# Sixteen of 31 convolution taps on TensorE in 32x32 tiles, on copies of the input turned by partitions

## The chip, the cores and the metric

One NeuronCore of a Trainium2 chip runs the whole program. The metric is the device time of one execution, in microseconds (us). Before the change it is 2149.69 us, the median of three runs (2148.77 to 2149.78).

## What is computed

Two stacked transformer blocks of different kinds, each two layers deep, over 256 tokens of width 1024, all in float32. What bears on the change is the mixer of the second block: its input projection gives queries, keys, values, a convolution input `c` (two halves of 512 channels) and gates. The convolution is depthwise, with 31 taps over the tokens, and a layer norm and a silu follow.

```python
        q, k, v, c, g = jnp.split(u @ w_in[i], splits, axis=-1)
        ...
        c = depthwise_conv(c, conv_w[i], conv_b[i])     # 31 taps, 512 channels, padding 15 on both sides
        c = jax.nn.silu(layer_norm_2(c, conv_ln_g[i], conv_ln_b[i]))
        y_conv = c @ w_conv_out[i]
        ...
        h = h + (g_attn * y_attn + g_conv * y_conv) @ w_o[i]
```

The input of the taps is the gated product of the two halves of `c`.

## The kernel before

Activations lie with features on the partitions and the 256 tokens along the free dimension, 128 features to a tile. Weights stream from HBM in blocks of eight 128x128 tiles (`raw`, 512 KB). Seven blocks are loaded ahead by SP; ScalarE rounds a block to its high half (`hi`), five blocks ahead of TensorE, and VectorE subtracts for the low half (`lo`), four ahead. A projection of 128 rows takes three matmuls for each weight tile (lo by high input, hi by high input, hi by low input).

The order of all work is written out by hand: `main_order` lists items, and every engine's program walks the same list. Side work is woven in by `Flow`: after each block of eight tiles, each engine calls `tick`, which takes one step ("next" to "next") of every chain that runs beside the main work. `tick` goes over the chains last in, first out; `chain(..., True)` puts one at the other end. The chains in this stage are the convolution (`conv2_steps`) and the attention (`att2_steps`: two pairs of heads, each scores, maxima, exponentials, division, transposes called `turn`, and `out`). In a chain's step every engine does its own part, so a step's place is tied to a block number on all engines.

In the second block's mixer the items are `c` 0 to 3 (each two columns of tiles), `conv2` (starts the chain after `c` 2), `c last`, `rcol`, `qkv` 0 to 2, `v2`, `qk norm`, `attention2` (starts that chain), eight `gate2`, four `attn out`, four `conv out`, four `wo`. VectorE makes the gated input, `Cb` (four tiles of 286 columns, zeros at both ends), from ScalarE's tanh. `CV` = 20 of the 31 taps are done on VectorE, one scalar_tensor_tensor of 256 columns each, accumulated in `cacc`. The other 11 are done on TensorE: ScalarE scales the identity by a tap's weights (`diag`, a ring of eight), TensorE multiplies the shifted `Cb` tile by it in float32 and accumulates in bank 4, and VectorE adds the bank to `cacc` (`conv sum`). A tick in the convolution chain has two taps on VectorE for each of two tiles, three diagonals on ScalarE, and three taps on TensorE, for two pairs of tiles in turn. Then come the mean, squares, variance, norm, silu and split, one tick each.

The attention of this stage uses the PSUM banks `ATT2` = (5, 6, 7, 2); the main items use `MAIN` = (0, 1, 3). A bank is waited for when it is taken (`take`) until its last reader has freed it.

In the first block, `quarters` multiplies in 64x64 tiles. It is quoted since the prediction reads its rows:

```python
                    for n in range(4):
                        for g, s in ((0, 0), (0, 1), (1, 0), (1, 1)):
                            rows, into = (slice(64 * t, 64 * t + 64) for t in (s, s ^ g))
                            h = 2 * n + g
                            i = pe.mm(outs[g][into, n * w:(n + 1) * w], left(h, rows), right(h, rows), True, True)
```

## Time and profile before

| | |
|---|---|
| median of three runs | 2149.69 us |
| the profiled execution | 2149.16 us, span 2147.4 us |
| TensorE matmul busy | 2120.1 us (99%) |
| VectorE busy | 1680.6 us (78%) |
| ScalarE busy | 1265.4 us (59%) |
| GpSimd busy | 13.1 us (1%) |
| DMA | 415 MB, mean 193 GB/s |

PE is TensorE's matmul, PEld its weight load, DVE VectorE, ACT ScalarE, POOL GpSimd, SP the engine that issues most DMAs. Times in rows are microseconds from the span's start unless marked ns; L198 and the like are lines of the kernel, and since helpers record every operation, a row is told by its tiles. A matmul's record goes on to the end of its pipeline, so that records overlap, and rates are read from start to start. "x6" in a timeline row is six instructions merged.

### The profile page before, as it was taken

The page shows a single profiled execution, that of the slowest core. Times are in us where ns is not written, and L with a number is a line of the kernel's source. Part 1 is how long each engine was busy: PE and PEld are TensorE (multiplying, and loading weights), DVE is VectorE, ACT ScalarE, POOL GpSimd, SP SyncE. Part 2 cuts the span into 40 slices and gives each one's busy share as a digit, 9 for nine tenths or more (in the row PEclk, how much of TensorE's full clock was granted, in tenths as well). Part 3 has the DMA queues.
Part 4 walks back from the last instruction along what each step waited for, and adds up shares of the span by engine and source line. Part 5 has one row for each costly group of instructions (what it writes and reads, how often), then busy time and mean ns, then how long its engine had stood idle before and what let it go on. Part 6 is the DMA issues. An engine that isn't in the chain of part 4 may idle for free.

```text
span 2147.4 us, 38873 instructions
## 1 busy us (share of the span) xinstructions
PE 2120.1 (99%) x16094; PEld 1934.2 (90%) x16094; DVE 1680.6 (78%) x2642; ACT 1265.4 (59%) x2122; POOL 13.1 (1%) x20
## 2 busy tenths in 40 slices
PE   8999999999999999999999999999999999999999
PEld 7898989999998899998888999888898889998888
DVE  7888698887877698776886677887688767878875
ACT  4765556555855755555655567665466545766554
POOL 0000000000000000000000000000000000000000
PEclk9999999999999999999999999999999999999999
DMA  9555577777644477555555533555555553346554
GB/s 371 192 194 174 173 244 258 240 244 276 215 158 168 158 253 231 186 186 186 180 193 187 168 117 132 203 191 191 187 177 191 192 186 128 124 164 205 191 191 129
DMA packets 116371, 415.12 MB, mean 193 GB/s; under 512 B 13105, under 2 KB 16561, under 8 KB 115682
## 3 DMA queue, kind: packets, MB, share of 16 engines
q1 hardware_dynamic: 116194, 412.63, 57.0%
q8 instruction: 127, 2.08, 0.4%
q14 instruction: 50, 0.41, 0.1%
HBM read 409.42 MB, written 3.16 MB: 192 GB/s over the span
## 4 chain that ended last, share of the span: by engine, by line
PE 91%; ACT 4%; DVE 3%; DMA 1%; issue 1%; SPq 0%; ACTq 0%; DVEq 0%
PE bank L198 90%; ACT arena L250 2%; DMA raw<-W 1%; DVE arena L205 1%; DVE lo L205 1%; ACT hi L250 1%; PE bank L202 1%; DVE ada L222 0%; ACT L250 0%; DVE arena L213 0%; ACT L242 0%; DMA xT<-x 0%; DVE h L205 0%; DVE ysl L205 0%; SPq L195 0%
## 5 line engine op out<-in xcount | busy, mean ns | idle before, releaser
L198 PE MATMUL bank<-h,hi 128*128 128x256 f32 (+1 forms) x5344 | 1223.0, 314 | 0.0
L250 ACT ACTIVATE hi<-raw 128x1024 fp32r<-128x1024 f32 x656 | 689.2, 1056 | 563.0 <-PE bank L198 500.7
L198 PE MATMUL bank<-h,lo 128*128 128x256 f32 x3440 | 986.1, 287 | 3.5 <-DVE h L205 3.5
L198 PEld LDWEIGHTS bank<-h,hi 128*128 128x128 f32 x5344 | 880.1, 190 | 67.1 <-issue 2.6
L205 DVE TENSOR_TENSOR lo<-raw,hi 128x1024 fp32r<-128x1024 f32 x656 | 793.1, 1220 | 90.7 <-ACT hi L250 89.8
L198 PEld LDWEIGHTS bank<-h,lo 128*128 128x128 f32 x3440 | 654.6, 190 | 15.1 <-issue 7.0
L198 PE MATMUL bank<-act,hi 128*128 128x512 f32 x1056 | 370.0, 393 | 0.0
L198 PE MATMUL bank<-act,lo 128*128 128x256 f32 x1056 | 294.7, 279 | 0.0
L198 PEld LDWEIGHTS bank<-act,hi 128*128 128x128 f32 x1056 | 197.9, 187 | 47.1
L198 PEld LDWEIGHTS bank<-act,lo 128*128 128x128 f32 x1056 | 197.9, 187 | 0.0
L250 ACT ACTIVATE arena<-arena 128x256 f32<-128x256 f32 (+4 forms) x202 | 98.5, 493 | 158.6 <-DVE arena L205 151.2
L250 ACT ACTIVATE arena<-bank 128x256 f32<-128x256 f32 (+3 forms) x428 | 173.6, 449 | 11.7 <-PE bank L198 10.1
L198 PE MATMUL bank<-arena 64*64 64x64 f32 (+7 forms) x2674 | 165.7, 272 | 7.0 <-ACT arena L250 3.9
L198 PEld LDWEIGHTS bank<-arena 64*64 64x64 f32 (+3 forms) x2674 | 123.6, 145 | 30.1 <-issue 8.5
L205 DVE TENSOR_TENSOR arena<-arena 128x256 f32<-128x256 f32 (+2 forms) x222 | 117.8, 535 | 20.7 <-ACT arena L250 16.9
L213 DVE SCALAR_TENSOR_TENSOR arena<-arena,par 128x256 f32<-128x256 f32 x260 | 116.0, 486 | 19.4 <-ACT arena L250 16.2
L205 DVE TENSOR_TENSOR act<-arena,act 128x256 fp32r<-128x256 f32 x132 | 56.0, 424 | 84.3 <-ACT act L250 83.9
L222 DVE CUSTOM_DVE_ANT_0 ada<-ada,crow,par 128x1024 f32<-128x1024 f32 x80 | 103.5, 1293 | 0.6 <-DMA ada<-WA 0.4
L205 DVE TENSOR_TENSOR arena<-bank,arena 128x256 f32<-128x256 f32 (+2 forms) x181 | 68.7, 423 | 3.6 <-ACT arena L250 3.6
L213 DVE SCALAR_TENSOR_TENSOR xT<-bank,xT 128x256 f32<-128x256 f32 x96 | 40.6, 422 | 35.1 <-PE bank L198 33.5
L250 ACT ACTIVATE act<-arena 128x256 fp32r<-128x256 f32 x132 | 52.9, 401 | 4.8 <-DVE arena L205 4.8
L198 PE MATMUL bank<-ysh,lo 128*128 128x256 f32 x192 | 55.6, 289 | 0.0
(150 smaller groups left out, 1891.6 us busy)
## 6 DMA issues: line engine op xcount, KB each, us to landing
raw<-W SPq DMA_DIRECT2D x664, 512.0 KB, 3.3
ada<-WA SPq DMA_DIRECT2D x80, 512.0 KB, 3.6
arena<-WA SPq DMA_DIRECT2D x16, 512.0 KB, 14.1
p_projected<-arena SPq DMA_DIRECT2D x2, 1024.0 KB, 7.3
arena<-scr SPq DMA_DIRECT2D x16, 128.0 KB, 4.7
arena<-p_projected SPq DMA_DIRECT2D x2, 1024.0 KB, 4.8
xT<-x SPq DMA_DIRECT2D x2, 512.0 KB, 4.9
arena<-lora SPq DMA_DIRECT2D x2, 512.0 KB, 10.3
```

What stands on the lines that cost most here:

```text
L198: return self.done(lambda e: e.matmul(out, l, r, start=start, stop=stop, skip_group_check=True))
L202: return self.done(lambda e: e.transpose(out, in_, ident[0:n, 0:n]))
L205: return self.done(lambda e: e.tensor_tensor(out, a, b, op))
L213: return self.done(lambda e: e.scalar_tensor_tensor(out=out, in0=a, scalar=s, in1=b, op0=o0, op1=o1))
L222: return self.done(lambda e: e.tensor_tensor_reduce(out, a, b, 1.0, start, MUL, ADD, total))
L250: return self.done(lambda e: e.activation(out, in_, f, scale=scale, **kw))
```

## The change

`CV` falls from 20 to 15, so 16 taps go to TensorE. Each 128x128 diagonal becomes four 32x32 ones. A tap has a turn d = 0 to 3, counted through in order of the taps: its four matmuls take partitions 32r to 32r+31 of a copy of `Cb` that is turned by d quarters, and write partitions 32c, c = (r+d) mod 4, of the bank of that turn. Four taps in a row have four turns, and so use all sixteen pairs of row and column group. Turn 0 is `Cb` itself; the other three copies are made by six DMAs for a pair of tiles, issued on ScalarE (`turned`). The diagonals are built on the host and loaded in each layer, 1 MB (`tapw`, at `mixer2`, on SP), and ScalarE builds none. On TensorE the taps are no longer woven into the ticks: two items `taps`, one for each pair of tiles, come after `rcol` and after `qkv` 0, each of 2 tiles x 16 taps x 4 matmuls, into the four banks of `ATT2`. `qkv` goes in the order 2, 0, 1. VectorE adds four banks for each pair (`conv sum`, two at a tick). The convolution chain still has 20 ticks before `conv total`. On VectorE `gate2` waits for the second `taps`, as its output lies where the copies lay. On ScalarE the attention's chain is no longer put first in the list.

```diff
-CW, CV = 31, 20
+CW, CV = 31, 15
+CG = 4
+CT, CS = CW - CV, 128 // CG
...
+def tap_turn(m, n):
+    return (m % 2 * CT + n) % CG
...
+    s = [("taps", 0, 0, 4), "next", ("taps", 0, 4, 8), "next", ("conv sum", 0, 0), "next", ("conv sum", 0, 2), "next"]
+    s += [("taps", 2, 0, 4), "next", ("conv sum", 2, 0), "next", ("conv sum", 2, 2), "next"]
+    for pair, n in ((0, 8), (2, 4)):
+        while n < 2 * CV:
+            s += [("taps", pair, n, min(n + 4, 2 * CV)), "next"]
+            n += 4
...
-        s += [("mixer2", l), ("c", l, 0), ("c", l, 1), ("c", l, 2), ("conv2", l), ("c", l, 3), ("c last", l), ("rcol", l)]
-        s += [("qkv", l, p) for p in range(3)] + [("v2", l), ("qk norm", l), ("attention2", l)]
+        s += [("mixer2", l), ("c", l, 0), ("c", l, 1), ("c", l, 2), ("turned", l, 0), ("conv2", l), ("c", l, 3), ("c last", l)]
+        s += [("turned", l, 2), ("rcol", l), ("taps", l, 0), ("qkv", l, 2), ("qkv", l, 0), ("taps", l, 2), ("qkv", l, 1)]
+        s += [("v2", l), ("qk norm", l), ("attention2", l)]
...
-        diag = [un(61, 4)[:, i * 128:(i + 1) * 128] for i in range(8)]
+        Ct = [Cb] + [ar[:, 73 * 256 + i * 1144:73 * 256 + (i + 1) * 1144].rearrange("p (m t) -> p m t", m=4) for i in range(CG - 1)]
+        tapw = un(20, 8)[:, 0:4 * CT * CS].rearrange("p (m n i) -> p m n i", m=4, n=CT)
...
+                elif what == "taps":
+                    l, pr = q
+                    outs = [take(ATT2, ("conv", l, pr, d)) for d in range(CG)]
+                    pe.wait_ge(d_taps, ("taps", l))
+                    pe.wait_ge(d_turn[pr // 2], ("turned", l, pr))
+                    pe.wait_ge(v_main, ("c", l, pr + 1))
+                    for m in (pr, pr + 1):
+                        for n in range(CT):
+                            d = tap_turn(m, n)
+                            for r in range(CG):
+                                c = (r + d) % CG
+                                rows, into = slice(CS * r, CS * r + CS), slice(CS * c, CS * c + CS)
+                                i = pe.mm(t256(outs[d], m - pr)[into, :], tapw[rows, m, n, :], Ct[d][rows, m, CV + n:CV + n + 256],
+                                          (m - pr) * CT + n < CG, False)
+                    i.then_inc(pe_main, ("conv", l, pr))
...
                     elif what == "conv sum":
...
+                        v.wait_ge(pe_main, ("conv", l, pr))
+                        for d in range(first, first + 2):
+                            use = ("conv", l, pr, d)
+                            v.wait_ge(v_cv, before[pr])
+                            v.tt(o, o, ps(use), ADD).then_inc(v_cv, use, frees=use)
...
                     v.wait_ge(pe_main, item)
+                    v.wait_ge(pe_main, ("conv", l, 2))
...
+                elif what == "turned":
+                    l, pr = q
+                    a.wait_ge(v_main, ("c", l, pr + 1))
+                    for d in range(1, CG):
+                        n = CS * d
+                        for out, src in ((slice(0, 128 - n), slice(n, 128)), (slice(128 - n, 128), slice(0, n))):
+                            a.dma(Ct[d][out, pr:pr + 2, :], Cb[src, pr:pr + 2, :]).then_inc(d_turn[pr // 2], item)
...
-                    f.chain(("att2", q[0]), att2_steps(q[0]), attention2(q[0]), True)
+                    f.chain(("att2", q[0]), att2_steps(q[0]), attention2(q[0]))
...
+                elif what == "mixer2":
+                    l = q[0]
+                    s.wait_ge(pe_main, ("f down 1", l, 7))
+                    s.dma(tapw.rearrange("p m n i -> p (m n i)"), T["taps"][l]).then_inc(d_taps, ("taps", l))
```

## Rows read from the trace of the kernel before

**Rows 1.** The page: busy time, and the chain that ended last by engine.

```profile
PE 2120.1 (99%) x16094; PEld 1934.2 (90%) x16094; DVE 1680.6 (78%) x2642; ACT 1265.4 (59%) x2122; POOL 13.1 (1%) x20
...
PE 91%; ACT 4%; DVE 3%; DMA 1%; issue 1%; SPq 0%; ACTq 0%; DVEq 0%
```

**Rows 2.** Who TensorE waited for: total us, times, longest.

```profile
PE bank L198 <- ACT arena L250: 8.7, 9, 2.9
```

**Rows 3.** Busy time by stretch: us, then PE, PEld, DVE, ACT, POOL, clock, DMA.

```profile
1262.00:1300.00 38.00, 38.00 (x288) 34.89 (x287) 35.12 (x64) 27.69 (x65) 0.00 (x0) 1.00 0.34 112
```

**Rows 4.** Groups by shape, TensorE: the taps' form (count | busy us, mean ns).

```profile
L198 PE MATMUL bank<-arena 128*128 128x256 f32 x192 | 47.5, 381 | 0.0
```

**Rows 5.** Timeline of TensorE, layer 0 (start us, us): main tiles, taps, transposes.

```profile
1204.48 0.28 PE L198 MATMUL bank<-h,lo 128*128 128x256 f32 x1
...
1204.84 0.28 PE L198 MATMUL bank<-h,lo 128*128 128x256 f32 x1
...
1249.61 2.31 PE L198 MATMUL bank<-arena,cst 128*128 128x512 f32 x6
...
1254.63 1.46 PE L198 MATMUL bank<-arena 128*128 128x256 f32 x6
...
1269.95 1.46 PE L198 MATMUL bank<-arena 128*128 128x256 f32 x6
1274.11 1.46 PE L198 MATMUL bank<-arena 128*128 128x256 f32 x6
...
1282.44 1.91 PE L202 MATMUL bank<-cst,arena 128*128 128x128 f32 x16
```

**Rows 6.** Timeline of TensorE: small tiles of `quarters`, and of the scores.

```profile
191.79 1.16 PE L198 MATMUL bank<-arena 64*64 64x64 f32 x64
...
1261.85 0.40 PE L198 MATMUL bank<-h,hi 128*128 128x256 f32 x2
1262.18 2.00 PE L198 MATMUL bank<-arena 64*128 64x256 f32 x16
1264.11 0.39 PE L198 MATMUL bank<-h,lo 128*128 128x256 f32 x1
```

**Rows 7.** Timeline of VectorE: keys, lo, taps, score sums, bank sum, maxima.

```profile
1253.91 1.68 DVE L213 SCALAR_TENSOR_TENSOR arena<-arena,par 128x1024 f32<-128x1024 f32 x2 [8.10 <-ACT arena L250]
1255.51 1.22 DVE L205 TENSOR_TENSOR lo<-raw,hi 128x1024 fp32r<-128x1024 f32 x1
1256.64 1.67 DVE L213 SCALAR_TENSOR_TENSOR arena<-arena,par 128x256 f32<-128x256 f32 x4
...
1263.34 2.48 DVE L213 SCALAR_TENSOR_TENSOR arena<-bank,arena 128x512 f32<-128x512 f32 x4 [0.58 <-PE bank L198]
1265.74 0.68 DVE L205 TENSOR_TENSOR arena<-arena,bank 128x512 f32<-128x512 f32 x1
...
1268.91 2.28 DVE L225 TENSOR_REDUCE sml<-arena 128x8 f32<-128x2048 f32 x1
```

**Rows 8.** Timeline of ScalarE: first of eight exponentials, next hi, eight scalings.

```profile
1273.04 0.49 ACT L250 ACTIVATE arena<-arena,sml 128x256 f32<-128x256 f32 x1
...
1276.98 1.04 ACT L250 ACTIVATE hi<-raw 128x1024 fp32r<-128x1024 f32 x1
...
1278.81 3.29 ACT L250 ACTIVATE arena<-arena,sml 128x256 f32<-128x256 f32 x8
```

**Rows 9.** Timeline: VectorE's gated product of `c` 1, and TensorE's `rcol`.

```profile
1217.29 0.43 DVE L213 SCALAR_TENSOR_TENSOR arena<-arena 128x256 f32<-128x256 f32 x1 [0.76 <-ACT arena L250]
...
1221.48 0.60 PE L198 MATMUL bank<-cst,rs_t 1*128 1x1 f32 x4
```

**Rows 10.** Weight loads: KB and us to landing; and min/median/max ns of an issue.

```profile
raw<-W SPq DMA_DIRECT2D x664, 512.0 KB, 3.3
...
L195 SPq DMA_DIRECT2D raw<-W x664: 327/328/1405, 4.1 to 2121.9; - x166
```

**Rows 11.** Timeline of TensorE: the variance of the convolution's norm.

```profile
1322.38 0.67 PE L198 MATMUL bank<-arena,cst 128*128 128x256 f32 x2 [0.99 <-DVE arena L205]
```

More of the change, by code:

```diff
@@ L355, in conv2_steps @@
 def conv2_steps(l):
-    s = []
-    for pair in (0, 2):
-        todo = [(m, j) for m in (pair, pair + 1) for j in range(CV, CW)]
-        built = []
-        for j in range(0, CV, 2):
-            s += [("taps", pair, j)]
-            if j >= 4:
-                s += [("pe tap", pair, *t) for t in built.pop(0)]
-            built.append(todo[:3])
-            del todo[:3]
-            s += [("diag", pair, *t) for t in built[-1]] + ["next"]
-        assert not any(built), built
-        s += [("conv sum", pair)]
-    return s + ["next", ("mean",), "next", ("square",), "next", ("var",), "next", ("norm",), ("silu",), "next", ("split",)]
+    s = [("taps", 0, 0, 4), "next", ("taps", 0, 4, 8), "next", ("conv sum", 0, 0), "next", ("conv sum", 0, 2), "next"]
[4 more added lines that the diff above has]
+            n += 4
+    return s + [("conv total",), "next", ("mean",), "next", ("square",), "next", ("var",), "next", ("norm",), ("silu",), "next", ("split",)]
 LN_STEPS = [("stats",), "next", ("sqrt",), "next", ("recip",), "next", ("norm",)]
@@ L504, in build @@
         d_x = [signal(f"dma_x{i}", 16) for i in range(2)]
+        d_turn = [signal(f"dma_turned{i}", 16) for i in range(2)]
         d_hank = [signal(f"dma_hank{i}", 16) for i in range(8)]
@@ L1040, in conv2 @@
             def conv2(l):
[L1041 removed]
                 def step(what, *q):
[L1044 to L1054 removed]
+                    if what == "mean":
                         o = take(CONV, ("cmean", l))
@@ L1658, in conv2 @@
             def conv2(l):
+                before, last_use = {}, {}
                 def w(m, j):
@@ L1663, in step @@
                     if what == "taps":
-                        pr, j0 = q
-                        for j in range(j0, min(j0 + 2, CV)):
-                            for m in (pr, pr + 1):
-                                o = t256(cacc, m)
-                                if j == 0:
-                                    v.wait_ge(v_main, ("c", l, m))
-                                    x = v.ts(o, Cb[:, m, 0:256], w(m, 0), P("conv_b_2", l, m), MUL, ADD)
-                                else:
-                                    v.wait_ge(v_cv, ("tap", l, m, j - 1))
-                                    x = v.stt(o, Cb[:, m, j:j + 256], w(m, j), o, MUL, ADD)
-                                x.then_inc(v_cv, ("tap", l, m, j))
+                        pr, first, last = q
@@ new lines, in step @@
+                        for n in range(first, last):
+                            j, m = n // 2, pr + n % 2
+                            o = t256(cacc, m)
+                            if j == 0:
+                                v.wait_ge(v_main, ("c", l, m))
+                                x = v.ts(o, Cb[:, m, 0:256], w(m, 0), P("conv_b_2", l, m), MUL, ADD)
+                            else:
+                                v.wait_ge(v_cv, last_use.pop(pr) if pr in last_use else ("tap", l, m, j - 1))
+                                x = v.stt(o, Cb[:, m, j:j + 256], w(m, j), o, MUL, ADD)
+                            x.then_inc(v_cv, ("tap", l, m, j))
+                            before[pr] = ("tap", l, m, j)
@@ new lines, in step @@
+                        for d in range(first, first + 2):
+                            use = ("conv", l, pr, d)
+                            v.wait_ge(v_cv, before[pr])
+                            v.tt(o, o, ps(use), ADD).then_inc(v_cv, use, frees=use)
+                            before[pr] = last_use[pr] = use
+                    elif what == "conv total":
+                        v.wait_ge(v_cv, ("tap", l, 3, CV - 1))
+                        v.tt(cy2[:, 0:512], cacc[:, 0:512], cacc[:, 512:1024], ADD).then_inc(v_cv, ("conv half", l))
+                        v.wait_ge(v_cv, ("conv half", l))
+                        v.tt(cy2[:, 0:256], cy2[:, 0:256], cy2[:, 256:512], ADD).then_inc(v_cv, ("conv total", l))
@@ L2332, in conv2 @@
                 return step
-            conv_taps = [(m, j) for pr in (0, 2) for m in (pr, pr + 1) for j in range(CV, CW)]
             def merge(name, l, m, h):
@@ L2928, in stream, with tap_weights @@
     return out.reshape(nblk, 128, BT * 128)
+def tap_weights(inputs):
+    w = np.asarray(inputs["conv_w_2"], np.float32).reshape(L, CW, 4, CG, CS)
+    out = np.zeros((L, CG, CS, 4, CT, CS), np.float32)
+    i = np.arange(CS)
+    for m in range(4):
+        for n in range(CT):
+            for r in range(CG):
+                out[:, r, i, m, n, i] = w[:, CV + n, m, (r + tap_turn(m, n)) % CG, :]
+    return out.reshape(L, 128, 4 * CT * CS)
 def modulation(inputs):
```

44 lines of the change are left out of this document (7 added, 37 removed).

## The prediction

> **What bounds the kernel now.** Read the page's busy line and its chain first: TensorE is busy 99% of the span and holds 91% of the chain that ended last [rows 1]. The view of who waited for whom says how little TensorE ever waits: its largest entry is 8.7 us in 9 times, outside this stage [rows 2]. The table by stretches shows the same in the stage that changes (the second block's mixer, from its "c" projections to "conv out", 1197 to 1323 us in layer 0, and again in layer 1): TensorE has no idle time there at the full granted clock, VectorE 92% busy in the attention part [rows 3]. So time taken off TensorE counts in full, until VectorE or ScalarE is late for it. Where that point lies is the larger part of the work below.
>
> **TensorE, what goes.** A tap is one float32 matmul with a diagonal as weights, and the trace shows two records for each call: 3 taps of a step stand as x6. 88 taps give 176 of the 192 records of this form [rows 4]. In the timeline two such bursts start 4.16 us apart; a block of eight weight tiles without one takes 8 x 0.36 = 2.88 us (start to start of its lo matmuls), so a burst costs 1.30 us, 0.217 a record, 0.434 a tap [rows 5]. 44 taps a layer: 19.1 us, all on the path.
>
> **TensorE, what comes.** Each `taps` item issues 2 x 16 taps x 4 tiles = 128 calls, 256 records of 256 columns, two items a layer. A record occupies its tile as long as before, 0.217 us; what matters is how many tiles run at once. The trace has no 32-row tile. It has 64x64 ones in the very pattern of the change (`quarters`: rows s into columns s, then rows s into columns s^1 of another bank): 64 records in 1.16 us [rows 6], (1.16-0.22)/63 = 14.9 ns each. One alone would take 217/4 = 54 ns, so four run at once. The scores, two row tiles of 256 columns, take (2.00-0.39)/15 = 107 ns a record, half of 217. Sixteen tiles at once would want 217/16 = 13.6 ns a record. I take the densest seen, 14.9: 256 x 14.9 = 3.8 us, and 0.3 us for entry and return, as the scores show (last hi before them at 1261.97, so the next was due at 1262.09; the next came at 1264.11: 2.02 us against 16 x 0.108) [rows 6]. So 4.1 us an item, 8.2 a layer; TensorE's own work falls by 10.9 us a layer. Bounds of an item: 3.8 us (13.6 ns) and, if only a tap's own four tiles run together, 64 x 0.217 + 0.3 = 14.2 us.
> The Trainium skill speaks against this change here: "TensorEngine Tiling (Array Packing)", Gotcha 1, says that different row tiles cannot access the same PSUM bank simultaneously, and a tap's four row tiles all write the bank of their turn. The trace disagrees for tiles that write different partitions: `quarters` writes one bank from both row halves and keeps 14.9 ns. For the other side, "TensorE: Matmul & The Clock Gate", Part 3, gives 10.6 times for sixteen tiles; no run here shows it, and nothing below rests on it.
>
> **The new waits of `taps`.** The first item needs the turned copies. Their input is ready at 1217.7, after VectorE's step at 1217.29; TensorE reaches the item after `rcol`, at 1222.0 [rows 9], 4.3 us later. In between ScalarE issues six copies (a DMA issue takes 0.33 us on SP, so 2.0 us) and they land: a 512 KB load lands in 3.3 us [rows 10], these six move 0.86 MB beside such loads. Estimate 4.8 us from ready to landed, bounds 3.5 and 7: a stall of 0.6 us a layer (0 to 2.7). ScalarE stands 2 us at these issues; behind it in its queue is the next hi split, and TensorE waits for that split's lo only four blocks (11 us) later. The second item comes 14 us after the copies can start and waits for nothing; its banks come from VectorE's sums one block earlier. The 1 MB load of the diagonals on SP waits for what the next weight load waits for anyway, and is used 20 us later; seven blocks are ahead of it: nothing. The added wait of VectorE in `gate2` is for work long done.
>
> **VectorE and ScalarE.** VectorE loses 20 tap steps a layer (0.40 each, from 1.6 for four) and gains six sums of 512 columns (0.6 each) [rows 7]: -4.4 us. ScalarE loses 44 diagonals (0.29 each), -12.8, gains 4 us of issue. Neither is on the path by itself, but both feed the attention, whose steps are tied to TensorE's blocks: `scores`, then five blocks later `turn`, which needs the probabilities. Before, those blocks carried bursts; now they don't, and TensorE arrives too early. I step the three in-order queues with start-to-start times of the rows [rows 7, 8] (lo 1.13, four taps 1.6, product 0.6, four score sums 2.4, maxima and sink 2.9, eight exponentials 4.1, eight scalings 3.2).
> Chain to the first `turn`, from the start of `qk norm`'s matmuls (1249.61): 6.0 us to the normed keys (1253.91+1.68); then VectorE's queue 1.13+1.6+1.13+1.6+0.6+1.13+2.4 = 9.6 to the scores' sums; 1.6+1.13+2.9 = 5.6 to the maxima; 1.6+0.6+1.13+0.8+1.13+0.3 = 5.6 to the reciprocals (the exponentials run beside it in 4.1); 3.2 on ScalarE. Sum 30.0 us. TensorE's way there is 1.9 for `qk norm`, eight blocks and the scores, 1.9+23.0+1.8 = 26.7; before, 26 tap records (5.6; four bursts of six and one of two, the first at 1254.63) made it 32.3, and it arrived at 1282.44 for a result of 1282.1 [rows 5, 8]. The difference is 3.3; with the hand-over between engines at each of the steps I take a stall of 3.8 us.
> Chain to the second `turn`, from the second scores: 2.5+1.6+1.13+2.9+0.6+1.6+0.6+1.13+1.6+1.13+0.3+3.2 = 18.3 against 5 x 2.88+1.75 = 16.15: 2.2 us. The wait before the convolution's variance (0.99 us [rows 11]) and 0.2 us at the second scores go, since the convolution's last steps come in the same block numbers as before and TensorE got there late.
> Per layer: -10.9 + 0.6 + 3.8 + 2.2 - 1.2 = -5.5. Two layers: **-11.0 us**. The same stepping of the kernel before lands on its 0.99 wait and within 0.2 us of its first maxima, so I give the stall terms +-1 us each, 4 us over both layers.
>
> **Sum.** The profiled execution took 2149.16 us (span 2147.4), the median is 2149.69, 0.5 above. 2149.2-11.0 = 2138.2; I say 2138.5.
>
> **Rivals.**
> (a) Half the tiles at once, 8 (27 ns a record, 7.2 us an item), or the same loss by another way: the instruction stream is dense (512 loads and matmuls an item, where the trace has at most 128 together) and the copies land 2 us later than taken. For: nothing in the trace runs more than four tiles, and each call is two passes on its own tile, so sixteen at once wants 62 instructions looked past. Against: with four tiles the second passes did not block the third and fourth tile. Eight at once: an item +3.1 us, a layer +6.2, so +0.7 a layer against before: 2150.6. A milder form (0.6 us for sixteen calls, an item 5.1 us, and copies 1.2 us later) gives -5.5+2.0+1.2 = -2.3 a layer, 2144.6.
> (b) Slower: one tap at a time, four tiles. Its place is the `taps` item, 14.2 us, its price 2 x (14.2-4.1) = 20.2 us a layer, +40.4 against the forecast and +29.4 against before: 2178.6. An item decides against the change from 4.1+2.75 = 6.9 us on, 8 tiles or fewer at once. For: a tap's row tiles share one bank; that is the skill's rule, named above. Against: `quarters` does the same in pairs at full rate [rows 6].
> (c) The stalls at `turn` don't come, because VectorE and ScalarE run ahead of what I stepped: -10.9+0.6-1.2 = -11.5 a layer at best: 2126.2. Against: the first maxima need 2.9 us on VectorE after four 0.6 us sums, and none of this is shortened. Half of it gives 2132.4.
>
> **How the numbers follow.** Forecast (12 tiles or more at once, stalls as stepped, 2134 to 2144): 0.57. (a) with both forms, 2144 to 2153: 0.21. (b) 0.14. (c) 0.08. The range leaves out (b) and the far half of (c): 2133 to 2153. A measurement of this kernel tells about 0.2% (4.3 us) from no change: faster is the forecast, (c) and a little of (a); same is most of (a); slower is (b) and (a)'s tail: 0.66, 0.18, 0.16.
>
> **What would show it.** `taps` matmuls (32*32) as four groups of 256 records, 3.8 to 4.1 us each; 7 us would be (a), 14 us (b). TensorE idle before the transposes of `turn`, 3.8 and 2.2 us in each layer, released by ScalarE's scalings; under 1 us before the first `taps`, released by a DMA. Period of a block in the attention part 2.88 instead of 4.16 us. VectorE's gaps before the maxima gone. I am wrong if a `taps` group is over 5 us, if the `turn` waits are absent, or if weight tiles (lo) come late.

## The result, and the profile after

The changed kernel takes 2168.15 us (median, 2167.18 to 2170.28) against 2149.23 us before: a ratio of 1.0091 with a 95% interval of 1.0079 to 1.0103. It is slower by 0.9%, where 2138.5 us had been forecast. Its profiled execution took 2168.52 us, with a span of 2166.6 us, 19.2 more than before's 2147.4.

The page of after, busy time and the chain that ended last:

```profile
PE 2111.4 (97%) x16942; PEld 1921.1 (89%) x16942; DVE 1672.0 (77%) x2614; ACT 1240.4 (57%) x2034; POOL 13.1 (1%) x20
...
PE 83%; DVE 7%; ACT 6%; DMA 2%; issue 1%; ACTq 1%; SPq 0%; DVEq 0%
```

TensorE is busy for 8.7 us less than in [rows 1], in a span 19.2 us longer: so it stands 28 us more. The chain says the same: TensorE's share falls from 91% to 83%, and VectorE, ScalarE and a DMA take it over. Who TensorE waited for, in after (total us, times, longest):

```profile
PE bank L204 <- ACT sml L256: 18.8, 2, 9.7
PE bank L204 <- ACT arena L256: 8.7, 9, 2.9
PE bank L208 <- ACT arena L256: 8.0, 4, 3.0
```

The second line is the one of [rows 2], unchanged. The first is new, two waits, one a layer, and larger than all else; the third is `turn`, four waits. The timeline of TensorE in layer 0 and layer 1 of after (start us, us; in brackets the idle time before it and its releaser; "issue" where the profile shows nothing that was waited for):

```profile
1223.18 0.60 PE L204 MATMUL bank<-cst,rs_t 1*128 1x1 f32 x4
...
1232.91 6.78 PE L204 MATMUL bank<-arena 32*32 32x256 f32 x256 [9.12 <-ACT sml L256]
...
1248.45 5.28 PE L204 MATMUL bank<-arena 32*32 32x256 f32 x256
...
1296.01 2.43 PE L208 MATMUL bank<-cst,arena 128*128 128x128 f32 x16 [3.02 <-ACT arena L256]
...
1321.90 1.94 PE L208 MATMUL bank<-cst,arena 128*128 128x128 f32 x16 [0.96 <-ACT arena L256]
...
1807.23 7.49 PE L204 MATMUL bank<-arena 32*32 32x256 f32 x256 [9.68 <-ACT sml L256]
...
1823.48 3.92 PE L204 MATMUL bank<-arena 32*32 32x256 f32 x180
1828.75 1.50 PE L204 MATMUL bank<-arena 32*32 32x256 f32 x67 [1.35 <-issue]
```

Between the end of `rcol` at 1223.8 and the first `taps` at 1232.9 TensorE stands for 9.1 us. `sml` is where ScalarE copies `rcol` to. ScalarE's timeline of after tells why it is so late:

```profile
1219.45 3.84 ACTq L201 DMA_DIRECT2D arena<-arena  x6
1223.39 2.00 ACT L256 ACTIVATE hi<-raw 128x1024 fp32r<-128x1024 f32 x2 [4.43 <-PE bank L204]
...
1227.92 0.42 ACT L256 ACTIVATE arena<-arena 128x256 f32<-128x256 f32 x1 [2.22 <-DVE arena L211]
1228.83 3.76 ACTq L201 DMA_DIRECT2D arena<-arena  x6
1232.64 0.17 ACT L256 ACTIVATE sml<-bank 128x2 f32<-128x2 f32 x1 [4.30 <-issue]
```

`rcol` holds bank 2. The first `taps` takes all four banks of `ATT2 = (5, 6, 7, 2)`, so it needs bank 2. The copy that frees it (0.17 us, the last row) stands in ScalarE's queue behind `turned` 2, which waits for the last gated product and then issues six DMAs for 3.8 us. A copy of two columns became the end of a chain, because one bank more was asked for and six issues stood ahead of it.

While TensorE stands, its clock goes. Stretches of after (start:end, us, TensorE busy and records, granted clock, DMA share, GB/s):

```profile
1220.00:1224.00 4.00, 3.78 (x32) 1.00 0.81 233
1224.00:1228.00 4.00, 0.00 (x0) 0.71 0.97 255
1228.00:1232.00 4.00, 0.00 (x0) 0.50 0.42 121
1232.00:1236.00 4.00, 3.09 (x101) 0.52 0.45 115
1236.00:1240.00 4.00, 4.00 (x177) 1.00 0.01 4
...
1296.00:1300.00 4.00, 3.99 (x25) 0.67 0.02 6
```

In layer 0 the granted clock falls to 0.50 (1.2 GHz) when TensorE has stood 1.9 us and is still there for three us of work behind the wait; the same happens, shorter, behind the 3.0 us at the first `turn`. Before has 1.00 throughout both mixers. After has 10.2 us at half clock around the first wait of layer 0 (3.0 of them with work), 3.4 us around its first `turn`, and 13.7 us around the wait of layer 1 (5.5 with work).

For all comparisons below one measure is used beside the time: how much longer than before the stretch of a mixer takes in the profiled execution, from the hi split that starts at 1194.5 in before to the one at 1346.2 (layer 0), and from 1765.7 to 1915.7 (layer 1), the same splits found by their number in every trace. It leaves out what else differs between two executions (up to 1.7 us ahead of the mixer).

| kernel | time us | ratio to before, 95% | layer 0 | layer 1 |
|---|---|---|---|---|
| after | 2168.15 | 1.0091 [1.0079, 1.0103] | +7.9 | +9.3 |
| `rcol` ahead of `turned` 2 | 2161.51 | 1.0051 [1.0036, 1.0066] | +2.6 | +4.7 |
| `rcol` ahead of `c last` (the *neighbour* below) | 2158.36 | 1.0047 [1.0030, 1.0063] | +1.8 | +5.2 |
| neighbour, one turn | 2179.49, one run | | +15.2 | +15.6 |
| neighbour, half the columns | 2157.62, one run | | +3.4 | +5.6 |
| neighbour, half the calls | 2152.78, one run | | +1.5 | +2.4 |
| neighbour, short taps on VectorE | 2154.46, one run | | -0.1 | +3.5 |
| neighbour, the word put back | 2160.71, one run | | +5.1 | +7.1 |
| `taps` behind one block more | 2157.09 | 1.0037 [1.0024, 1.0049] | +1.8 | +4.9 |
| behind three blocks | 2150.22 | 1.0006 [0.9997, 1.0015] | -0.7 | +3.2 |
| that, `turn` a block later | 2170.47 | 1.0101 [1.0084, 1.0118] | +8.0 | +11.5 |
| three blocks, three taps a block | 2148.65 | 0.9999 [0.9989, 1.0009] | -3.3 | +0.4 |
| that, `turn` a block later | 2144.34 | 0.9986 [0.9977, 0.9995] | -2.9 | -2.7 |

Where the median and the stretches differ by some us, the kernel's own runs do: the last one's eleven lie between 2142.0 and 2149.8, while before's fifteen beside it lie between 2147.3 and 2149.3.

### The profile page after: what moved, and what is told of

Its sections match the earlier page's. It is cut to its first block, busy times and chain, and to the rows that moved or that the text cites. A ratio compares the mean times of both kernels' runs of the same rounds, so it can differ in the third digit from the quotient of the medians.

```text
span 2166.6 us, 40483 instructions
## 1 busy us (share of the span) xinstructions
PE 2111.4 (97%) x16942; PEld 1921.1 (89%) x16942; DVE 1672.0 (77%) x2614; ACT 1240.4 (57%) x2034; POOL 13.1 (1%) x20
## 4 chain that ended last, share of the span: by engine, by line
PE 83%; DVE 7%; ACT 6%; DMA 2%; issue 1%; ACTq 1%; SPq 0%; DVEq 0%
PE bank L204 83%; ACT arena L256 4%; DVE lo L211 2%; DMA raw<-W 2%; DVE arena L219 2%; ACT hi L256 1%; DVE arena L211 1%; PE bank L208 1%; ACTq L201 1%; ACT L256 0%; DMA xT<-x 0%; DVE sml L231 0%; DVE m L211 0%; DVE h L211 0%; ACT L248 0%
## 5 line engine op out<-in xcount | busy, mean ns | idle before, releaser
L204 PE MATMUL bank<-arena 64*64 64x64 f32 (+6 forms) x3522 | 147.6, 317 | 27.1 <-ACT sml L256 18.8
L204 PEld LDWEIGHTS bank<-arena 64*64 64x64 f32 (+3 forms) x3522 | 110.8, 133 | 51.5 <-issue 20.7
L219 DVE SCALAR_TENSOR_TENSOR arena<-arena,par 128x256 f32<-128x256 f32 (+1 forms) x220 | 99.4, 486 | 14.5 <-ACT arena L256 11.3
L211 DVE TENSOR_TENSOR arena<-arena,bank 128x256 f32<-128x256 f32 (+2 forms) x72 | 35.4, 491 | 45.5 <-PE bank L204 43.8
## 6 DMA issues: line engine op xcount, KB each, us to landing
arena<-arena ACTq DMA_DIRECT2D x8, 214.5 KB, 2.6
```

The costliest lines, as they stand in the source:

```text
L204: return self.done(lambda e: e.matmul(out, l, r, start=start, stop=stop, skip_group_check=True))
L211: return self.done(lambda e: e.tensor_tensor(out, a, b, op))
L219: return self.done(lambda e: e.scalar_tensor_tensor(out=out, in0=a, scalar=s, in1=b, op0=o0, op1=o1))
```

## The experiments

### Who holds the first `taps`

`rcol` ahead of `turned` 2, one swap in the order:

```diff
-        s += [("turned", l, 2), ("rcol", l), ("taps", l, 0), ...
+        s += [("rcol", l), ("turned", l, 2), ("taps", l, 0), ...
```

> The changed kernel with one swap in the order: `rcol` before `turned` 2, nothing else. Theory (bank 2): the first `taps` waits 9.1 and 9.7 us because its four banks include bank 2, which `rcol` holds until ScalarE has copied it out, and ScalarE's copy stands behind the six DMA issues of `turned` 2. With the swap the copy stands behind the last tanh of `c` only (1227.92 to 1228.34 in layer 0), and TensorE is at the first `taps` at 1223.8: a wait of 4.6 us, still released by ScalarE's copy (sml). Two layers save 2 x 4.8 = 9.6 us plus 1 to 3 us of half clock: 2156 to 2159 us. Rival (the turned copies land late, and the release shown is only the later of two): the wait stays over 8 us and is now released by a DMA; 2166 to 2169 us.

`rcol` ahead of `c last`, so that ScalarE doesn't wait for the last gate either:

```diff
-  ... ("c", l, 3), ("c last", l)]
-        s += [("turned", l, 2), ("rcol", l), ("taps", l, 0), ...
+  ... ("c", l, 3), ("rcol", l), ("c last", l)]
+        s += [("turned", l, 2), ("taps", l, 0), ...
```

> The changed kernel with `rcol` moved ahead of `c last`, so that ScalarE copies bank 2 out before it waits for the last gate. Theory (bank 2, then the copies): the copy runs at about 1225.8, and the next to come last are the turned copies of `turned` 0, issued from 1219.45 to 1223.3 and landing 2.6 to 3.5 us after issue, near 1226.5: the first `taps` waits 2 to 3 us, released by a DMA. Two layers save 2 x 6.8 = 13.6 us and 2 to 4 us of half clock: 2151 to 2155 us, which is still above the kernel before, since the items cost 5.3 us and not 4.1. Rival (the wait is not the whole loss, the order of ScalarE's and VectorE's steps is): the wait goes to under 3 us, but the time stays above 2160 us.

The first of these kernels, who TensorE waited for, and its first item:

```profile
PE bank L204 <- ACT sml L256: 9.4, 2, 4.8
...
1226.64 6.00 PE L204 MATMUL bank<-arena 32*32 32x256 f32 x204 [4.81 <-ACT sml L256]
1233.11 1.39 PE L204 MATMUL bank<-arena 32*32 32x256 f32 x52 [0.47 <-issue]
```

The swap halves the wait, from 18.8 to 9.4 us, as the theory had it to 0.2 us. Its profiled execution (2156.67 us) lies in the range; its median, 2161.5, is above it. The row names ScalarE's copy (`sml`, which ends at 1226.43), but the last of the turned copies lands at 1226.39 in the same trace: two holders, 0.04 us apart. In the second kernel ScalarE and then TensorE:

```profile
1217.19 3.83 ACTq L201 DMA_DIRECT2D arena<-arena  x6
1221.12 2.00 ACT L256 ACTIVATE hi<-raw 128x1024 fp32r<-128x1024 f32 x2 [4.42 <-PE bank L204]
...
1223.34 0.15 ACT L256 ACTIVATE sml<-bank 128x2 f32<-128x2 f32 x1
...
1226.26 7.22 PE L204 MATMUL bank<-arena 32*32 32x256 f32 x256 [4.73 <-ACT arena L256]
...
1793.99 8.20 PE L204 MATMUL bank<-arena 32*32 32x256 f32 x256 [4.80 <-DMA arena<-arena]
```

Bank 2 is free at 1223.5, and still TensorE stands until 1226.3. The row of layer 1 names the releaser, a DMA (in layer 0 the engine named had long been done): it is the turned copies. The last one lands at 1226.02 and at 1793.74, and in both layers the item starts 0.25 us later. The kernel below that has no copies and no wait for them stands 1.1 and 1.0 us here. VectorE's gated product of `c` 1 ended at 1217.16 in this trace, so the copies take 8.9 us from ready to landed, of which 3.8 are ScalarE's six issues at 0.64 us each; the last copy lands 5.6 us after its issue.

In after, too, the copies had landed at 1228.4 and 1803.5, 4.5 and 3.7 us before the item started. So two holders of the first `taps` lay one behind the other, and taking the later away brought the earlier to light. That is why both kernels are alike, and why the expectation of 2 to 3 us here was wrong. Their lateness goes with the traffic beside them: in after the last copy of the first set landed 5.7 us after its issue, with the DMA engines 81 to 97% busy, and that of the second set, while they were 42 to 45% busy, 2.6 us. No run changed that traffic alone.

### Does the cover help, and what comes behind it

`taps` behind `qkv` 2, and VectorE's sums of it one block later:

```diff
-("turned", l, 2), ("taps", l, 0), ("qkv", l, 2), ("qkv", l, 0), ("taps", l, 2), ("qkv", l, 1)
+("turned", l, 2), ("qkv", l, 2), ("taps", l, 0), ("qkv", l, 0), ("taps", l, 2), ("qkv", l, 1)
-... ("taps", 0, 4, 8), "next", ("conv sum", 0, 0), "next", ("conv sum", 0, 2), "next"]
+... ("taps", 0, 4, 8), "next", ("taps", 0, 8, 12), "next", ("conv sum", 0, 0), ("conv sum", 0, 2), "next"]
```

> On top of `rcol` ahead of `c last`: the first `taps` comes after `qkv` 2, and VectorE's sums of it one block later (three blocks of its own taps first, then both sums at once). The run with only `rcol` moved still waited 4.7 and 4.8 us at the first `taps`, and its item took 7.2 and 8.2 us, in part at half clock. Theory (what stands there now is the landing of the turned copies, 9 us after c1's product, and the half clock follows from standing still): `qkv` 2 covers 2.9 us of it, the wait falls to about 1.9 us, the clock stays full and the item takes 5.3 to 5.8 us: 2 x (2.9 + 1.7) = 9 us less than 2158.4, 2148 to 2151 us. Rival (the copies land later still, pushed by whatever TensorE does then, or VectorE's later sums hold the banks of the second item): the wait moves to the second `taps` or stays over 4 us, and the time stays above 2154 us.

The waits fell to 1.6 us as reckoned and to 3.1 us in layer 1, but the stretches hardly got shorter (+1.8 and +4.9), and the time is the rival's. Its reason isn't: no wait of over 4 us is left and none stands before the second `taps`. In layer 0 the waits, items and gaps sum to 2.0 us less than the neighbour's, and 3.4 us at half clock behind the first `turn`, which the neighbour hasn't, cost 1.7. Its gaps behind the taps, TensorE's timeline:

```profile
1227.79 3.91 PE L204 MATMUL bank<-arena 32*32 32x256 f32 x180 [1.61 <-ACT arena L256]
1232.40 1.96 PE L204 MATMUL bank<-arena 32*32 32x256 f32 x76 [0.70 <-issue]
...
1246.76 0.28 PE L204 MATMUL bank<-h,hi 128*128 128x256 f32 x1 [0.80 <-issue]
...
1311.07 0.70 PE L204 MATMUL bank<-arena,cst 128*128 128x256 f32 x2 [0.95 <-DVE arena L211]
```

`taps` 0 behind `qkv` 0 too, `taps` 2 behind `qkv` 1, and the sums in the blocks after each:

```diff
+("turned", l, 2), ("qkv", l, 2), ("qkv", l, 0), ("taps", l, 0), ("qkv", l, 1), ("taps", l, 2)]
+    for n in range(0, 20, 4):
+        s += [("taps", 0, n, n + 4), "next"]
+    s += [("conv sum", 0, 0), ("conv sum", 0, 2), "next", ("taps", 2, 0, 4), "next", ("conv sum", 2, 0), ("conv sum", 2, 2), "next"]
```

> Three blocks of projection (`qkv` 2 and `qkv` 0) between `c last` and the first `taps`, which itself stands ahead of `qkv` 1, the second behind it; VectorE's sums follow in the blocks after. With one block of cover the first `taps` still waited 1.6 and 3.1 us. Theory (the copies land 9 us after c1's product, and standing and half clock cost the rest): no wait ahead of either `taps`, items of 5.3 us (up to 7 where a piece of instructions comes late), the two waits ahead of `turn` of 3.0 and 1.0 us a layer stay: a layer takes 19.1 - 10.6 - 4.0 + 1.0 = 5.5 us less than before at best, 2 to 4 with the rest of the half clock: 2139 to 2146 us. Rival (what is saved ahead of the taps comes back behind them, as one block later it did: VectorE, whose taps and lo splits fill a block, is late with the sums, the transposes or the products behind): new waits released by VectorE of 3 us or more a layer, and 2150 us or more.

There is no wait ahead of either `taps` any more, and the time is that of before within 0.2%. It is 4 us above the theory. It is also the rival's time, but VectorE's new waits are 2.0 us a layer and not 3 or more. TensorE's timeline in this kernel:

```profile
1230.16 2.79 PE L204 MATMUL bank<-arena 32*32 32x256 f32 x132
1233.88 1.49 PE L204 MATMUL bank<-arena 32*32 32x256 f32 x66 [0.92 <-issue]
...
1285.38 1.94 PE L208 MATMUL bank<-cst,arena 128*128 128x128 f32 x16 [2.99 <-ACT arena L256]
...
1303.52 0.70 PE L204 MATMUL bank<-arena,cst 128*128 128x256 f32 x2 [0.53 <-DVE arena L211]
1313.20 0.67 PE L204 MATMUL bank<-arena,cst 128*128 128x256 f32 x2 [1.47 <-DVE arena L211]
...
1795.03 3.94 PE L204 MATMUL bank<-arena 32*32 32x256 f32 x183
1802.20 1.17 PE L204 MATMUL bank<-arena 32*32 32x256 f32 x32 [3.23 <-issue]
```

What is left is of two kinds: gaps "issue" inside the items (see the next part), and the waits at `turn`, the mean and the variance. In layer 0 items with their gaps take 13.4 us for 19.1, and stands of 3.0, 0.5 and 1.5 us are there for 1.0 before: -1.7, measured -0.7. In layer 1 the items take 15.7 us, 3.2 of them that gap: +0.6, and 3.4 us at half clock behind `turn` add 1.7; measured +3.2, so 0.9 us stay unexplained.

### Sixteen tiles, and what feeds them

All taps on the diagonal tiles (row tile equal to column tile, the unturned image), so that only four of the sixteen tiles are used for the same 256 records. The copies, their issues, TensorE's wait for them and the host's turning of the weights go too:

```diff
-                                c = (r + d) % CG
+                                c = r
-   ... tapw[rows, m, n, :], Ct[d][rows, m, CV + n:CV + n + 256],
+   ... tapw[rows, m, n, :], Ct[0][rows, m, CV + n:CV + n + 256],
```

> As the run with `rcol` ahead of `c last`, and all of TensorE's taps read the unturned image with their row tile equal to their column tile, so that only four of the sixteen tiles are ever in use; the number of instructions and columns is the same (the taps are then computed with wrong channels' weights left unrotated only in the sense that no copy is used). Theory (tiles that differ in row and column run at once; here each tile has every fourth instruction): the four diagonal tiles carry 64 records each, and a record of a tile can't overlap the next of the same tile: about 14.2 us an item at full clock (64 x 0.22 us), 2 x 2 x 9 = 36 us more than its neighbour, near 2188 us. Rival (an issue rate bounds both): the item stays at 5 to 6 us, and the time at 2150 to 2156 us.

```profile
1245.00 14.02 PE L204 MATMUL bank<-arena 32*32 32x256 f32 x256
```

The second item; all four are alike. 14.02 us is 64 x 0.219: rival (b)'s price to 0.2 us, but for the kernel that keeps to four tiles. The four records of a round start 7 ns apart, in four row tiles that write one bank. With turns the same 256 records take 5.28 us, so more than four tiles do run at once, 10 to 11 on average. The whole kernel took 2179.5 us and not the expected 2188; it also lacks 7.4 us of its neighbour's waits for copies. (The last words of the expectation on this kernel's weights are loose: it computes all taps.)

Half the columns, the same instructions (half the tokens get no share of TensorE's taps):

```diff
-... pe.mm(t256(outs[d], m - pr)[into, :], ..., Ct[d][rows, m, CV + n:CV + n + 256],
+... pe.mm(t256(outs[d], m - pr)[into, 0:128], ..., Ct[d][rows, m, CV + n:CV + n + 128],
```

> As the run with `rcol` ahead of `c last`, and TensorE's taps take 128 of the 256 columns (the other half of the tokens gets no share of these taps; work left out). Theory (the item is bound by the feeding of load and matmul pairs, some 19 ns a record, not by columns): an item stays at 4.9 to 5.4 us, and the time within 2 us of its neighbour. Rival (columns bound it, sixteen tiles being less than all at once): an item falls to 2.6 to 3 us, and the time by 8 to 10 us.

Half the instructions, the same columns (512 to a call; the second half of a pair gets the first's weights):

```diff
-                    for m in (pr, pr + 1):
+                    for m in (pr,):
-... pe.mm(t256(outs[d], m - pr)[into, :], ..., Ct[d][rows, m, CV + n:CV + n + 256],
+... pe.mm(outs[d].rearrange("p (m t) -> p m t", m=2)[into, :, :], ..., Ct[d][rows, m:m + 2, CV + n:CV + n + 256],
```

> On top of `rcol` ahead of `c last`: TensorE's taps as calls of 512 columns, both halves of a pair at once with the first half's weights (so the second half gets wrong weights): half the calls, the same columns. Theory (the item is bound by the supply of instructions: 256 loads and 256 matmuls an item, of which the trace shows pieces of 16 KB being fetched 3.5 to 3.9 us apart while an item runs): an item falls from 5.3 to 3.8 to 4.3 us, and the gap of 1.5 us inside the last one in layer 1 goes. Rival (columns or conflicts of tiles bound it): the item stays at 5.0 us or more.

The second item of layer 0 in these two kernels (5.28 us in their neighbour), first the one with half the columns:

```profile
1240.77 1.92 PE L204 MATMUL bank<-arena 32*32 32x128 f32 x130
1243.75 1.88 PE L204 MATMUL bank<-arena 32*32 32x128 f32 x126 [1.05 <-issue]
```

```profile
1241.07 4.47 PE L204 MATMUL bank<-arena 32*32 32x512 f32 x128
```

Half the columns save 0.4 us of 5.28 (and 0.7 of 7.3 in the last item of layer 1), and the time stays within 2 us of the neighbour's, as the theory had it. The theory's pace of 19 ns a record is wrong here, though: up to the gap records start 12.8 ns apart on average, against 18.3 in the neighbour, and the gap of 1.05 us takes most of that back. Half the instructions save 0.8 of 5.28, and 2.9 of 7.3 in layer 1, where the gap is gone; 4.47 is a little above the 3.8 to 4.3 expected. So both count: columns in the pace, and the number of instructions in the pace and in the gaps, which keep an item from getting much shorter. At pure columns on all sixteen tiles it would be 256 x 0.217 / 16 = 3.5 us; nothing here reached that.

Two things are in it. The first is pace: behind the first 32 records of the item (two to a tile), which start 6.7 ns apart in two groups of sixteen, records start 16.7 ns apart, with a break of some 0.15 us every 33 records; over the item it is 19.2 ns on average. With 512 columns the 16.7 ns stand there too and the breaks are longer, with 128 they nearly go. The second is supply. The trace lists the pieces in which instructions come, by DMA, 16 KB each; while projections run one comes in some 15 us, inside an item they follow in 3.3 to 4.5 us, and every gap "issue" inside an item ends 1.2 to 1.7 us after a piece has landed. The gaps sit at fixed places of the instruction stream. In the two kernels with `rcol` moved, a gap comes at record 204 of layer 0's first item; with one block (24 records) ahead of the item at 180; with three blocks at 132, which is 204 - 72. In layer 1 it moves from 254 to 183 by the same three blocks (1 record off). In the kernel of half columns the gaps at record 204 of the first item and 130 of the second have 52 + 72 + 130 = 254 records between them, and with three blocks ahead those at 132 and 211 have 124 + 48 + 211 = 383: two and three times 128 (to 2), which is the 16 KB of a piece at 64 bytes each for a load and a matmul (an estimate from these distances). The lengths go from 0.1 to 3.5 us, and at one place they differ too (0.1 to 0.9 us at record 132). Half the instructions left no such gap in any item. That the supply makes these gaps is worked out from places and times; no run moved the supply alone.

### Who makes `turn` wait

VectorE's taps but the first on 8 of 256 columns:

```diff
-                                x = v.stt(o, Cb[:, m, j:j + 256], w(m, j), o, MUL, ADD)
+                                x = v.stt(o[:, 0:8], Cb[:, m, j:j + 8], w(m, j), o[:, 0:8], MUL, ADD)
```

> On top of `rcol` ahead of `c last`: VectorE's taps of the convolution but the first take 8 of 256 columns (work left out: the convolution lacks them elsewhere). Theory (the four waits ahead of `turn`, 7.9 us in all, come from the attention chain standing behind VectorE's taps): they fall below 2 us in all, and the profiled time by 5 to 7 us against its neighbour's 2156. Rival (they come from ScalarE's steps, the exponentials and the scalings, and from the chain's own length in blocks): they stay at 6 us or more, and the time within 2 us.

```profile
1289.40 1.95 PE L208 MATMUL bank<-cst,arena 128*128 128x128 f32 x16 [0.86 <-ACT arena L256]
...
1313.65 1.95 PE L208 MATMUL bank<-cst,arena 128*128 128x128 f32 x16 [0.85 <-ACT arena L256]
```

3.0 and 1.0 us became 0.86 and 0.85: some 2.3 of a layer's 4.0 us are VectorE's taps. The rest ends with ScalarE's scalings; how much of it is ScalarE's work, and how much VectorE's other steps ahead of it, is not shown. The stretches shrink by 1.9 and 1.7 us. Neither side was right in full, and the saving of 5 to 7 us was not there.

The word that the change took from ScalarE's attention chain, put back:

```diff
-                    f.chain(("att2", q[0]), att2_steps(q[0]), attention2(q[0]))
+                    f.chain(("att2", q[0]), att2_steps(q[0]), attention2(q[0]), True)
```

> On top of `rcol` ahead of `c last`: the one word that the change took out of ScalarE's chain of attention is put back, so that its steps come behind those of the other chains in each block, as in the kernel before. Theory (ScalarE has hardly a step of the convolution left, so the order of its chains is without effect): waits ahead of `turn` within 0.5 us of 7.9 in all and the time within 2 us of its neighbour's. Rival (without it the changed kernel's attention is late by the modulation's steps): the waits grow by 1 us or more each.

The waits at `turn` stay (3.00 and 0.97 us), but the stretches grow by 3.3 and 1.9 us. The wait of [rows 11] is back in both layers:

```profile
1326.64 0.67 PE L204 MATMUL bank<-arena,cst 128*128 128x256 f32 x2 [0.99 <-DVE arena L211]
```

So ScalarE's order is not without effect, which was the theory; that wait is 1.0 us of it. The rest can't be put down to the word: 3.4 us at half clock behind the first `turn` of layer 0 and a first `taps` that waits 5.9 us in layer 1 are there in kernels without it as well (half the columns, half the calls). The time itself, one run, lies among the neighbour's four (2156.0 to 2163.1).

`turn` one block later, first on top of the three blocks of cover:

```diff
-... ("divide", p), "next", "next", ("turn", p), "next"]
+... ("divide", p), "next", "next"] + ["next"] * (1 - p) + [("turn", p), "next"]
```

> As the run with three blocks of cover, and the first `turn` of attention one block later in the order (one more `next` ahead of it in the list of steps; the second follows as before, so it comes later by a block too). Theory (the first `turn` waits 3.0 us, one block's 2.88 us and a little, and the second 1.0, so one block more gives ScalarE and VectorE the time): both waits go to 0.2 us or less, 4 us a layer and what half clock they brought: 6 to 9 us less than its neighbour, near 2135 us. Rival (the chain behind ends one block later, and `attn out` waits for it): the waits go, but one of 2 to 3 us released by ScalarE or VectorE comes ahead of the last `out` or of `attn out`, and the time stays within 2 us.

```profile
1302.38 0.70 PE L204 MATMUL bank<-arena,cst 128*128 128x256 f32 x2 [3.10 <-DVE arena L211]
1312.56 1.19 PE L204 MATMUL bank<-arena,cst 128*128 128x256 f32 x2 [3.75 <-DVE arena L211]
...
1328.65 0.58 PE L204 MATMUL bank<-ysh,lo 128*128 128x256 f32 x1 [2.62 <-DVE ysl L211]
```

The waits at `turn` are gone and 20 us are lost: TensorE stands 3.1, 3.8 and 2.6 us a layer at the convolution's mean and variance and at the attention's output. Neither side of the expectation had this. VectorE's timeline of this kernel, at the mean:

```profile
1297.77 2.28 DVE L231 TENSOR_REDUCE sml<-arena 128x8 f32<-128x2048 f32 x1
...
1301.18 1.14 DVE L211 TENSOR_TENSOR arena<-arena 128x512 f32<-128x512 f32 x2
```

The reduction for the second half of the heads now ends 1.1 us ahead of the convolution's total (the two rows; 3.6 us ahead in the kernel with `turn` in its old place), and the mean on TensorE (1302.38) waits for that total. But this meeting is not where most is lost. Counted from the start of the mixer, TensorE comes to the variance after 119.5 us, and after 119.3 with `turn` in its old place: up to there it stands at the mean and the variance instead of at `turn`, and the second `turn` (1.9 us) is still to come. Of the 8.7 us that layer 0 loses, some 6 to 7 lie behind the variance: 6.8 us at half clock from 1311.4 on, and then the stand at the attention's output, with 3.4 us at half clock. ScalarE's and VectorE's rows ahead of that stand:

```profile
1325.81 0.63 ACT L256 ACTIVATE ych<-arena 128x512 fp32r<-128x512 f32 x1
...
1327.29 0.58 ACT L256 ACTIVATE ysh<-bank 128x512 fp32r<-128x512 f32 x1
...
1327.90 0.69 DVE L211 TENSOR_TENSOR ysl<-bank,ysh 128x512 fp32r<-128x512 f32 x1 [6.86 <-ACT ysh L256]
```

VectorE has long been idle there. It waits for `ysh`, ScalarE's high half of the attention's output, which now stands in ScalarE's queue behind the steps that make the convolution's (`ych`); with `turn` in its old place `ysh` came ahead of them. So the convolution's end had to move:

```diff
+        k = 3 if pair else 4
         while n < 2 * CV:
-            s += [("taps", pair, n, min(n + 4, 2 * CV)), "next"]
-            n += 4
+            s += [("taps", pair, n, min(n + k, 2 * CV)), "next"]
+            n += k
```

> As the run with three blocks of cover, and VectorE's taps of the second pair three to a block in place of four, two blocks longer: they then end where attention's load on VectorE is over. With four a block VectorE is without a pause from 1270 to 1303 us (four taps 1.66, a lo split 1.22, beside attention's 2.28 us reduction), while behind 1308 it stands 3.3 us at a time. Theory (the wait of 3.0 us ahead of the first `turn` and those of 0.5 and 1.5 us ahead of the convolution's mean and variance are VectorE's queue): they fall by 0.4 us for every block of the chain, to 1.5 to 2 us and under 0.5 us, and the time by 4 to 6 us, to 2144 to 2147 us. Rival (the first `turn` waits for ScalarE's exponentials and scalings, 3.0 us with whatever VectorE has): it stays at 3.0, the others go, and the time falls by 2 us at most.

The waits at `turn` are 2.2 and 0.85 us, and those at mean and variance are gone. The theory is right on the places, but 2.2 us is above its 1.5 to 2, and the time, within 0.1% of before, is above its 2144 to 2147. With both edits together:

> The run with three blocks of cover and three taps a block, and the first `turn` one block later, which with four taps a block made it 20 us slower (waits of 3.1, 3.8 and 2.6 us released by VectorE at the convolution's mean and variance and at the split of the attention output: the reduction for the second half of the heads, 2.28 us, met the convolution's total). Theory (it was this meeting; with three taps the total comes two blocks later and meets nothing): the waits ahead of `turn`, 2.2 and 0.9 us a layer, go, those three don't come back, and the time falls by 4 to 7 us from 2148.6: 2142 to 2145 us, the first version below the kernel before. Rival (VectorE has no block to spare in attention, whichever two steps meet): waits of VectorE of 3 us or more a layer in place of those of `turn`, and 2150 us or more.

```profile
1307.83 1.09 PE L204 MATMUL bank<-arena,cst 128*128 128x256 f32 x2 [1.80 <-DVE arena L211]
...
1801.12 1.93 PE L204 MATMUL bank<-arena 32*32 32x256 f32 x73 [3.48 <-issue]
```

One row of the waits that are left in layer 0, and one of layer 1. The ratio is 0.9986 [0.9977, 0.9995]: the first version below before, by some 3 us. Its median lies in the expected range. The reduction's end and the total are 6.3 us apart here, and ScalarE's `ysh` comes ahead of the convolution's steps again. The same "one block later" that cost 20 us with four taps a block saves some 3 us with three: 2.7 in the two stretches, and 2.8 by the ratios of the two kernels, whose intervals still overlap. The stands fall by 1.3 us in each layer; that layer 0 doesn't get shorter goes with 3.4 us at half clock, which lie in layer 0 of this kernel and in layer 1 of the one without the later `turn`. What is left are mainly the 1.8 us a layer of VectorE and the supply gap of 3.5 us in layer 1. Which of the meetings cost how much is read from the timelines; no run moved one step alone.

## Why the prediction was wrong

- **The new waits of `taps`, the step that failed.** It said 0.6 us for the first item, bounded by 2.7, and measured 9.1 and 9.7. The text asked only for the landing of the copies. It gave the banks a thought for the second item alone ("its banks come from VectorE's sums one block earlier"); that the first needs bank 2, which only ScalarE's copy of `rcol` frees, was not asked. And of what stands behind ScalarE's issues it named the hi split, not that copy, though both stand in the same few lines of the order. The swap of `rcol` shows it: 4.3 and 5.1 us of the two waits are this.
- **The copies, mis-sized.** 4.8 us from ready to landed, 7 at most; measured 8.9. The issue was taken from SP's row, 0.33 us [rows 10]; these copies on ScalarE take 0.64, 1.8 us more for the six. The rest is the landing of the last, 5.6 us after its issue, where 2.8 had been reckoned. So even without the bank the first item waits 4.7 us, above the bound of 2.7.
- **The item, mis-sized.** 14.9 ns a record and 4.1 us; measured 19.2 and 5.28 at full clock without a gap. Rival (a)'s milder form (5.1) had it nearly, and the sign of being wrong, a group over 5 us, is there. The dense instruction stream was named in (a) as a cause; half the calls bear it out. The gaps of up to 3.5 us were not foreseen. The four items of after sum to 26.8 us, against 16.4.
- **The clock.** No term of the sum had it. Before shows 1.00 in these stretches; after's clock falls while it stands, so the first items take 6.8 and 7.5 us, and the block products behind the first `turn` of layer 0 are slower too.
- **Right:** that the taps that go are worth 19.1 us a layer, as far as the sums below close (no run took them out alone); that more than four tiles run at once, so rival (b) was wrong (14.02 us only where four tiles are used), and with it the reading that four row tiles can't write one bank together. The Trainium skill's "TensorEngine Tiling (Array Packing)", Gotcha 1, would have it so; the runs don't agree for row tiles that write different partitions. In the kernel of one turn four of them write one bank at once, in rounds of 0.219 us, and with turns the item takes 5.28 us.
- **Right in kind:** the waits at `turn`, released by ScalarE's scalings, 3.0 and 1.0 us for 3.8 and 2.2. That the wait of [rows 11] goes is right; the reason given, the same block numbers, isn't the whole one, since with ScalarE's chains in the old order it is back. VectorE's work fell by 8.6 us and ScalarE's by 25.0, against 8.8 and 25.6 reckoned (without issues).

The terms, layer 0: -5.5 forecast, + 8.5 (wait), + 3.9 (items), - 2.0 (`turn`), + 0.5 (a gap behind the second item) = +5.4; measured +7.9. Of the rest 1.7 us are the 3.4 us at half clock behind `turn`. Layer 1: -5.5 + 9.1 + 6.5 - 2.0 = +8.1; measured +9.3. The last 0.8 and 1.2 us stay open. The wait is more than half of the miss: 17.6 of 30 us.

## What to carry to other kernels

Whoever takes one more bank or buffer for an item has to name, for each of them, its last holder, the instruction that frees it, and what stands ahead of that instruction in its own queue. Two waits can stand one behind the other with the same length, so after the first is found the next must be reckoned before a gain is promised. And when an engine is freed, the steps tied to its blocks come too early: the same shift of one block cost 20 us with four of VectorE's taps a block and saved some 3 with three, since it changes which steps of two chains stand behind one another, on ScalarE as well as on VectorE.

## What was not expected of the hardware

- TensorE's instructions come in pieces of 16 KB. 256 small loads and matmuls in 5 us use two pieces, and TensorE then often stands, for 0.1 to 3.5 us, in the middle of a burst, at a place fixed by the count of instructions ahead of it (the cause is worked out from places and times, see above).
- Sixteen 32x32 tiles: the first two groups of sixteen records start 6.7 ns apart, later ones 16.7, on average 19.2; with 128 columns instead of 256 it is 12.8 on average up to the gap.
- Four row tiles wrote four partition groups of one bank at once, at the full 0.219 us a round.
- Issues of these copies on ScalarE came 0.64 us apart, where a weight load's issue on SP took 0.33. The two differ in form too, so it isn't shown that the engine makes the difference. The last of the first six copies (71.5 to 214.5 KB each) landed 8.7 to 11.0 us after their input was ready.
- After TensorE had stood 4.6 us or more the granted clock was 0.50 (1.2 GHz) for the first us of the next work; a stand of 3.0 us at the first `turn` was at times followed by it too, and in the last kernel one of 1.8 us.
